# Two-layer attention and RWKV trunk on one core: RWKV's key norms and small functions made during the input projection, its small projections in pairs, its inputs finished tile by tile

## The chip, the cores and the metric

One Trainium2 chip, one NeuronCore. The time is device microseconds (us) of one launch of the whole program. Everything is float32. Shares of TensorE's clock are of 2.4 GHz: 1.00 in a row is 2.4 GHz, 0.50 is 1.2 GHz.

## The reference, cut to what matters

Two layers over T = 1040 tokens of width 1024 (kept transposed: 8 tiles of 128 partitions by W = 1044 columns). Each layer has one input projection `z = u @ w_in`, whose columns feed sparse attention (A) and RWKV-7 time mixing (B), an output projection, and an MLP. Part B's inputs, which the change is about:

```
zB = zB + (zB_prev - zB) * mu_l                  # token shift
r, k, v, xw, xa, xg = split(zB)                  # 512, 512, 512, 64, 64, 160 (+32 for v mixing in layer 1)
w = -softplus(-(w0 + tanh(xw) @ w2)) - 0.5;  decay = exp(-exp(w))
a = sigmoid(a0 + xa @ a2);   g = sigmoid(xg) @ g2
if layer 1: v = v + (v_first - v) * sigmoid(v0 + parts[6] @ v2)
kk = k * k_k;  kk = kk / max(norm(kk per head), 1e-12)
k = k * (1.0 + (a - 1.0) * k_a)
y = rwkv7_scan(r, decay, k, v, kk, kk * a)       # then group norm, bonus, gate by g
```

## The kernel before, in words

The program is written by hand, one instruction list per engine, with semaphores between them. A layer runs in this order: root mean square norm; the **projection**; **attention** by blocks of 128 queries; the **stage between** attention and the scan, which makes RWKV's inputs; the **scan** in 17 chunks of 64 tokens; the **stage behind** it (group norm, bonus, gate); the output projection; the MLP.

**Projection.** `z` has 24 tiles of 128 columns, called units u0 to u23; `ORDER` says which tile is made when. TensorE makes a unit with 24 matmuls (`unit`, 8 contraction tiles by 3 slices of 348 columns; each f32 matmul is two instructions in the trace) into three PSUM banks. There are two such triples of banks, used in turn by the list `ITEMS`, which holds the units and a few other products; an item waits until ScalarE has emptied the item two places before it (`tri_out`). ScalarE empties a unit that takes part in the token shift with two copies (`shifted`: one scaled by 1 - mu, one by mu into `stage`), and GpSimd adds the second, one token later, to the first (`add_shifted`).

Meanwhile VectorE searches the threshold of the 256 best keys per query, one bit at a time, 31 bits (`bit_step`): a few operations on 7 columns give the trial value (`trial_ready`), `count_ge` counts five blocks, and ScalarE counts the two longest ones (`sign_counts`: a Sign over 1024 and one over 1040 columns). ScalarE does its share of the bits behind certain units, by the table `BITS_AFTER` (2 or 3 bits behind each of units 12 to 19). ScalarE works in program order: while it waits for a bit it empties no PSUM.

Before the change u10 to u13 are the tiles of r, u14 to u17 k, u18 to u21 v, u22 the tile of xw and xa (`Z_LORA`), u23 that of xg. Attention may start when the last `add_shifted` is through (VectorE's wait on `z_ready`, then L1669 to L1673, then `attn_in`).

**Stage between.** All after attention (`attn_done`): VectorE scales k by k_k (L1722); ScalarE squares it (L1263) and makes tanh and two sigmoids (L1265 to L1269); TensorE makes four products for w (contraction over 64 rows, L974); then sums of squares per head (L985, 8 output rows); VectorE's max (L1737); ScalarE's inverse root as Ln and Exp (L1072, L1074); four products for a (64 rows) and in layer 1 four for v (32 rows); four products that spread the inverse norms over the head's rows (`one`, L671, 8 rows); VectorE multiplies (L1745), mixes v in layer 1 (L1735, L1749, L1750), and at the end treats k and kk over all four tiles at once (L1754, L1758, L1760). ScalarE empties each product with a sigmoid (L1279), two triples of banks in turn. The scan starts with ScalarE's L1142 (`scan_ready`).

**Stage behind.** Mean by blocks (L1007), squares, sums per head (L1015, the same 8-column selector), inverse root, bonus (L1025), gate (L1034 with 128 rows, L1036 with 32) and the spread of the inverse root (L1043, 8 rows). The selectors are loaded by DMA before each of the two stages (`heads_in`).

## Time and profile before

| | us |
|---|---|
| Median of 3 runs | 4003.57 (4001.94 to 4006.88) |
| The profiled execution, its own time | 3997.3 |
| Its span, first to last instruction | 3995.5 |
| TensorE busy | 3693.6 (92%) |
| VectorE busy | 2082.3 (52%) |
| ScalarE busy | 902.5 (23%) |
| GpSimd busy | 563.0 (14%) |
| Mean granted clock of TensorE | 0.949 |

The shares are means over stages with different limits, so they don't tell what the change is worth. A wait row reads "engine, line <- who was waited for: total us, times, longest us". In the timeline, the bracket at a row's end is the engine's idle time just before it and who ended it.

### The profile page before, as it was taken

To read this page: it belongs to the slowest core of one execution; us is meant where nothing else is said; L and a number is where in the kernel's file an instruction comes from. 1 tells how busy PE (TensorE), PEld (TensorE's weight loads), DVE (VectorE), ACT (ScalarE), POOL (GpSimd) and SP (SyncE) were. 2 spreads that over 40 slices of the span, in tenths; PEclk is the share of its full clock that TensorE was granted. 3 is DMA by queue.
4 is the path that set the end of the run, shared out by engine and by line. 5 is a ranking of instruction groups with operands and counts; after the bars stand their busy time and mean duration, and the time that the engine had idled before them with its cause. 6 is when DMAs were issued, how large, how long until landed. Compare 5 with 4: busy or idle time off the path is not lost.

```text
span 3995.5 us, 68805 instructions
## 1 busy us (share of the span) xinstructions
PE 3693.6 (92%) x29040; PEld 2815.2 (70%) x29040; DVE 2082.3 (52%) x4090; ACT 902.5 (23%) x1765; POOL 563.0 (14%) x444
## 2 busy tenths in 40 slices
PE   7999887999979999999899998869999799999996
PEld 5565554996658888888655665559956588888885
DVE  2499745775153242434536997357751532434345
ACT  2345562332020000000124446523320200000000
POOL 0131100000012222222101310000000222222220
PEclk9999996998989999999999999869989899999998
DMA  3110110000211111112211111100002111111121
GB/s 117 30 42 32 46 22 1 4 4 26 74 55 47 46 44 43 43 43 85 85 41 32 37 33 24 33 2 4 4 26 75 64 43 42 43 43 43 43 85 54
DMA packets 44408, 165.75 MB, mean 41 GB/s; under 512 B 5568, under 2 KB 5584, under 8 KB 43744
## 3 DMA queue, kind: packets, MB, share of 16 engines
q1 hardware_dynamic: 28672, 102.82, 7.8%
q0 software_dynamic: 15456, 58.78, 4.0%
q8 instruction: 227, 3.72, 0.4%
q14 instruction: 53, 0.43, 0.0%
HBM read 135.01 MB, written 23.49 MB: 40 GB/s over the span
## 4 chain that ended last, share of the span: by engine, by line
PE 79%; DVE 14%; issue 3%; ACT 3%; POOL 1%; DMA 0%; DVEq 0%; ACTq 0%; POOLq 0%
PE ps L737 39%; PE ps L686 10%; PE ps L763 10%; PE ps L654 6%; DVE arena L1455 4%; PE ps L932 2%; PE ps L920 2%; PE ps L945 1%; PE ps L974 1%; DVE little L1485 1%; PE ps L698 1%; DVE arena L1351 1%; PE ps L664 1%; DVE arena L1358 1%; ACT arena L1240 1%
## 5 line engine op out<-in xcount | busy, mean ns | idle before, releaser
L737 PE MATMUL ps<-arena 128*128 128x261 f32 x4096 | 924.7, 383 | 3.9 <-POOL arena L573 2.9
L737 PEld LDWEIGHTS ps<-arena 128*128 128x128 f32 x4096 | 775.1, 189 | 133.3 <-issue 4.6
L686 PE MATMUL ps<-arena,ring 128*128 128x348 f32 x2304 | 702.6, 464 | 34.4 <-ACT arena L1113 20.7
L737 PE MATMUL ps<-arena,ring 128*128 128x261 f32 x3072 | 711.6, 387 | 15.1 <-DVE arena L1822 14.4
L737 PEld LDWEIGHTS ps<-arena,ring 128*128 128x128 f32 x3072 | 587.2, 192 | 119.3 <-issue 13.9
L686 PEld LDWEIGHTS ps<-arena,ring 128*128 128x128 f32 x2304 | 437.7, 192 | 299.1 <-issue 49.3
L763 PE MATMUL ps<-arena 64*64 64x64 f32 (+1 forms) x13600 | 475.6, 225 | 70.9 <-DVE arena L1536 43.2
L763 PEld LDWEIGHTS ps<-arena 64*64 64x64 f32 x13600 | 450.9, 135 | 91.6 <-issue 45.5
L1311 ACT ACTIVATE aux<-ps 128x522 f32<-128x522 f32 x64 | 38.9, 607 | 1527.6 <-PE ps L737 1527.6
L1397 DVE TENSOR_TENSOR arena<-aux,ps 128x522 f32<-128x522 f32 x160 | 111.8, 699 | 423.9 <-PE ps L737 423.4
L573 POOL TENSOR_TENSOR arena<-ring 128x512 f32<-128x512 f32 x128 | 172.4, 1347 | 1098.3 <-DMA ring<-units 1092.9
L1455 DVE TENSOR_SCALAR_CACHE_REDUCE arena<-arena,little 128x384 uint8<-128x384 f32 (+6 forms) x338 | 278.9, 885 | 11.2 <-DVE little L1479 11.0
L1397 DVE TENSOR_TENSOR arena<-arena,ps 128x522 f32<-128x522 f32 x200 | 139.8, 699 | 239.6 <-PE ps L737 237.1
L654 PE MATMUL ps<-arena,ring 128*128 128x348 f32 x768 | 228.5, 461 | 3.7 <-issue 3.7
L654 PEld LDWEIGHTS ps<-arena,ring 128*128 128x128 f32 x768 | 147.6, 193 | 85.6 <-issue 8.3
L1136 ACT ACTIVATE arena<-arena,little 128x1024 bf16<-128x1024 f32 x124 | 142.2, 1147 | 206.3 <-DVEq L1480 206.1
L546 POOL TENSOR_TENSOR arena<-arena 128x1043 f32<-128x1043 f32 x30 | 72.9, 2431 | 531.2 <-ACTq L1115 531.2
L1154 ACT ACTIVATE arena<-ps 128x128 f32<-128x128 f32 x340 | 92.8, 277 | 231.1 <-PE ps L763 217.5
L1688 DVE CUSTOM_DVE_ANT_0 arena<-ps,arena 128x128 f32<-128x128 f32 (+7 forms) x130 | 94.0, 760 | 94.6 <-PE ps L920 84.6
L1340 DVE TENSOR_TENSOR aux<-arena 128x1044 f32<-128x1044 f32 x16 | 19.9, 1246 | 194.1 <-ACT arena L1097 194.1
L1402 DVE SCALAR_TENSOR_TENSOR arena<-arena 128x522 f32<-128x522 f32 (+1 forms) x96 | 101.9, 1062 | 14.5 <-DVE arena L1397 1.1
L1601 DVE TENSOR_TENSOR arena<-arena,ps 128x128 f32<-128x128 f32 x340 | 95.5, 286 | 24.2 <-PE ps L763 23.8
(217 smaller groups left out, 3530.6 us busy)
## 6 DMA issues: line engine op xcount, KB each, us to landing
ring<-units SPq DMA_DIRECT2D x192, 512.0 KB, 3.7
h_scratch<-arena POOLq DMA_DIRECT2D x24, 522.0 KB, 3.3
arena<-h_scratch POOLq DMA_DIRECT2D x24, 522.0 KB, 8.0
arena<-h_in POOLq DMA_DIRECT2D x16, 522.0 KB, 9.9
out<-arena POOLq DMA_DIRECT2D x8, 522.0 KB, 3.2
arena<-att_scratch POOLq DMA_DIRECT2D x2, 2080.0 KB, 9.1
att_scratch<-arena POOLq DMA_DIRECT2D x16, 256.0 KB, 3.0
aux<-rope POOLq DMA_DIRECT2D x2, 1044.0 KB, 12.3
```

Source lines behind the costliest of these rows:

```text
L573: nc.gpsimd.tensor_tensor(w_sum(p, i), x, y, op).then_inc(S["weights_ready"], 1)
L654: ins = mm(ps[:, b + s, 0:SW], ring[:, (u % RING) * D + k * P:(u % RING) * D + (k + 1) * P], rhs(g * KT + k)[:, slice_(s)], start=(g == 0 ...
L686: ins = mm(ps[:, b + s, 0:SW], ring[:, r * D + k * P:r * D + (k + 1) * P], tile(U0, k)[:, slice_(s)], start=(k == 0), stop=(k == KT - 1))
L737: ins = mm(acc_at(n)[:, s], lhs[:, k * P:(k + 1) * P], rhs(k)[:, s * HALF:(s + 1) * HALF], start=(k == 0), stop=(k == KT // 2 - 1))
L763: ins = mm(out[r:r + HEAD], lhs[r:r + HEAD], rhs[r:r + HEAD], start=start, stop=stop)
L1136: go(signs[j][0:n], sc(b)[0:n], ACT.Sign, bias=negated[0:n, j:j + 1], scale=1.0, accum_out=sel[0:n, c:c + 1]).then_inc(S["signs_counted"], 1)
L1154: go(cb("x", 256)[:, P * half:P * (half + 1)], ps[:, half, 0:P], ACT.Copy).then_inc(S["x_out"], 1)
L1397: do(v.tensor_tensor(o, x, y, ALU.add))
L1402: do(v.scalar_tensor_tensor(x, x, 0.0, x, ALU.max, ALU.mult))
L1455: v.tensor_scalar(junk[j % 3][0:n, 0:SEL_W[b]], sc(b)[0:n], trial[0:n, c], None, ALU.is_ge, ALU.add, accum_out=count[0:n, c]).then_inc(S[" ...
L1601: v.tensor_tensor(mt, mt, bank2(2, 5, half), ALU.subtract).then_inc(S["mt_ready"], 1)
L1688: v.tensor_tensor_reduce(sm[u % 2][r][:, 0:k], flat[:, c:c + k], mask, -HEAD ** -0.5, 3.0e38, ALU.add, ALU.min, stat[:, at:at + 1])\
```

## The change

- The order of the units: u10 is the tile of xw and xa, u11 that of xg, u12 to u15 are k, u16 to u19 v, u20 to u23 r.
- Behind unit 13's bits ScalarE makes tanh and the sigmoids; behind those of units 14 to 17 it squares k (scaled by k_k, into the room of r). A new item "kk" behind u18 (`pair_sums`, 12 matmuls of 32 output rows, tile g into PSUM rows 32g to 32g+31) sums the squares per head; ScalarE copies it out behind unit 18's bits, VectorE takes the max behind the bits of unit 18, ScalarE makes the inverse root behind unit 20's copies.
- Between attention and the scan, each tile g: the products for w (rows 0 to 63) and a (rows 64 to 127) alternate into banks 0 to 2 and 3 to 5; the inverse norm is spread in two halves of 522 columns into banks 6 and 7, from 32 rows; VectorE makes kk from k, k_k and PSUM in one operation per half, scans the decay, and scales k and a; the factor 1 + (a - 1) k_a moves to ScalarE.
- The selectors (`selectors`, 128 by 160) lie in SBUF for good: a third DMA before h is loaded, and the two `heads` DMAs of each layer go. The stage behind uses them too, with 32 rows where 8 were.

```diff
-ORDER = [Z_KI, Z_QI, Z_QI + 1, Z_MISC, Z_C, Z_C + 1, *range(Z_Q, NZ)]
+ORDER = [Z_KI, Z_QI, Z_QI + 1, Z_MISC, Z_C, Z_C + 1, *range(Z_Q, Z_R), Z_LORA, Z_XG, *range(Z_K, Z_LORA), *range(Z_R, Z_K)]
-         *(f"u{n}" for n in range(9, NZ)))
+         *(f"u{n}" for n in range(9, 19)), "kk", *(f"u{n}" for n in range(19, NZ)))
...
+            def pair_sums(l):
+                b = tri_bank("kk")
+                pe.wait_ge(tri("kk"), tri_out(l, "kk") - 1)
+                pe.wait_ge(S["kk_sq"], 4 * (l + 1))
+                for s in range(SLICES):
+                    for g in range(4):
+                        ins = mm(of_pair(ps, g)[:, b + s, 0:SW], pair_sum, z(Z_R + g)[:, slice_(s)], start=True, stop=True)
+                ins.then_inc(S["virt_done"], 1)
...
+                    if n == 18:
+                        pair_sums(l)
...
+                for g in range(4):
+                    if g:
+                        pe.wait_ge(S["lora_out"], outs + 2 * g)
                     for s in range(SLICES):
-                        ins = mm(ps[:, b + s, 0:SW], a, x[:, slice_(s)], start=True, stop=True)
+                        for b, h in ((0, slice(0, 64)), (SLICES, slice(64, P))):
+                            ins = mm(ps[:, b + s, 0:SW], ax("w2a2")[h, g * P:(g + 1) * P], z(Z_LORA)[h, slice_(s)],
+                                     start=True, stop=True)
                     ins.then_inc(S["lora_ready"], 1)
+                    for half in range(2):
+                        if g or half or l:
+                            pe.wait_ge(S["kk_out"], 8 * l + 2 * g + half)
+                        for j in range(2):
+                            at = half * SPLIT + j * HALF
+                            ins = mm(ps[:, 6 + j, 0:HALF], of_pair(selectors, g)[:, PAIR:PAIR + P],
+                                     of_pair(kk_rows, g)[:, at:at + HALF], start=True, stop=True)
+                        ins.then_inc(S["kk_ready"], 1)
...
+                    if n == 13:
+                        act.wait_ge(S["z_ready"], mixed(11))
+                        go(z(Z_LORA)[0:64], z(Z_LORA)[0:64], ACT.Tanh)
+                        go(z(Z_XG), z(Z_XG), ACT.Sigmoid)
+                        go(z(Z_MISC)[0:32], z(Z_MISC)[0:32], ACT.Sigmoid).then_inc(S["lora_in"], 1)
+                    if 14 <= n < 18:
+                        g = n - 14
+                        act.wait_ge(S["z_ready"], mixed(K_UNIT + g))
+                        go(z(Z_R + g), z(Z_K + g), ACT.Square, scale=par(l, "kk", g)).then_inc(S["kk_sq"], 1)
+                    if n == 18:
+                        act.wait_ge(S["virt_done"], virt_at(l, "kk"))
+                        go(thirds(kk_rows), banks(tri_bank("kk")), ACT.Copy).then_inc(tri("kk"), 1)
...
+                    if n == 20:
+                        act.wait_ge(S["kk_max"], w.next("kk_max"))
+                        inverse_root(kk_rows, kk_rows, 0.0, 1).then_inc(S["root_ready"], 1)
...
+                for g in range(4):
+                    act.wait_ge(S["lora_ready"], w.next("lora_ready"))
+                    for b, dst, name in ((0, X_S0, "w0"), (SLICES, X_A0, "a0")):
+                        go(thirds(tile(dst, g, W, ZW)), banks(b), ACT.Sigmoid, bias=par(l, name, g), scale=1.0)\
+                            .then_inc(S["lora_out"], 1)
+                    act.wait_ge(S["lora_out"], outs + 2 * g + 2)
+                    go(yv(g), tile(X_A0, g, W, ZW), ACT.Identity, scale=par(l, "ka", g), bias=omka[:, g:g + 1])\
+                        .then_inc(S["ka_ready"], 1)
...
                 for g in range(4):
+                    kk, s, a, k = (tile(base, g, W, ZW) for base in (X_KK0, X_S0, X_A0, Z0 + Z_K * ZW))
+                    for half in range(2):
+                        part = slice(half * SPLIT, (half + 1) * SPLIT)
+                        dve.wait_ge(S["kk_ready"], w.next("kk_ready"))
+                        v.scalar_tensor_tensor(halves(kk[:, part]), halves(k[:, part]), par(l, "kk", g), ps[:, 6:8, 0:HALF],
+                                               ALU.mult, ALU.mult).then_inc(S["kk_out"], 1)
+                    scan = tile(X_S0, g, ZW, ZW)
+                    dve.wait_ge(S["lora_out"], outs + 2 * g + 1)
+                    v.tensor_tensor_scan(scan, const("reset"), scan, 0.0, ALU.mult, ALU.add).then_inc(S["dve_done"], 1)
...
+                    v.tensor_tensor(k, k, yv(g), ALU.mult).then_inc(S["keys_scaled"], 1)
+                    v.tensor_tensor(a, a, kk, ALU.mult).then_inc(S["dve_done"], 1)
```

**VectorE, from the end of attention (L1716, in the changed kernel L1740) to the first chunk.** Before:

```order
L1716 TENSOR_TENSOR arena<-ps,arena 128x512
L1722 TENSOR_SCALAR arena<-arena,prm 128x1088 x4
L1724 TENSOR_SCALAR little<-prm 128x4
L1729 MEMSET arena 128x44
L1730 SCALAR_TENSOR_TENSOR arena<-cst,arena 128x1088
L1737 TENSOR_SCALAR arena<-ps 8x1044
L1741 MEMSET arena 128x4x44
L1745 TENSOR_TENSOR arena<-arena,ps 128x1044 x4
L1754 TENSOR_SCALAR arena<-arena,prm,little 128x1044 x4
L1758 TENSOR_TENSOR arena<-arena 128x4x1044
L1760 TENSOR_TENSOR arena<-arena 128x4x1044
```

(The L1729 and L1730 rows stand there four times.) Now, the first tile of four and the end:

```order
L1740 TENSOR_TENSOR arena<-ps,arena 128x512
L1748 MEMSET arena 128x4x44 x2
L1754 SCALAR_TENSOR_TENSOR arena<-arena,prm,ps 128x522 x2
L1758 SCALAR_TENSOR_TENSOR arena<-cst,arena 128x1088
L1762 TENSOR_TENSOR arena<-arena 128x1044
L1763 TENSOR_TENSOR arena<-arena 128x1044
L1765 MEMSET arena 128x4x44
L1777 MEMSET arena 128x256
```

The four passes over all tiles have become one pass per tile, and the max over the sums is gone from here.

**ScalarE, in the projection of the changed kernel, from behind unit 13's bits to the copies of unit 15.** L1114 and L1118 are the two copies of a unit, L1141 the Signs, L1239 to L1241 tanh and sigmoids, L1245 a square:

```order
L1239 ACTIVATE arena<-arena 64x1044
L1240 ACT_TABLE_LOAD
L1240 ACTIVATE arena<-arena 128x1044
L1241 ACTIVATE arena<-arena 32x1044
L1114 ACTIVATE arena<-ps,arena 128x1044
L1118 ACTIVATE arena<-ps,prm 128x1044
L1141 ACTIVATE arena,little<-arena,little 128x1024
L1141 ACTIVATE arena,little<-arena,little 16x1040
L1141 ACTIVATE arena,little<-arena,little 128x1024
L1141 ACTIVATE arena,little<-arena,little 16x1040
L1245 ACTIVATE arena<-arena,prm 128x1044
L1114 ACTIVATE arena<-ps,arena 128x1044
```

Before, L1109 and L1113 (the copies) and L1136 (the Signs) stood there alone, in the same order. The Signs behind the sigmoids need no table of their own.

**TensorE, in the projection of the changed kernel, from unit 9 on.** L683 are the units' matmuls, 24 to a unit, L714 the pair sums:

```order
L683 MATMUL ps<-arena,ring 128x348 x240
L714 MATMUL ps<-arena,selectors 32x348 x12
L683 MATMUL ps<-arena,ring 128x348 x120
L929 MATMUL ps<-arena 128x128 x4
```

Before it was one row of 360 (units 9 to 23): the pair sums now stand between unit 18 and unit 19.

## Rows read from the trace of the kernel before

**Rows 1.** The page's first line.

```profile
span 3995.5 us, 68805 instructions
```

**Rows 2.** Chain that ended last, layer 0: start, length, what.

```profile
568.30 1.92 PE ps L920 x8
...
590.15 10.43 issue
600.58 14.27 PE ps L974 x24
...
616.06 9.54 PE ps L985 x24
...
640.02 14.30 PE ps L671 x24
...
949.32 7.13 PE ps L1015 x24
```

**Rows 3.** Timeline: both layers' stage between, its first and last row.

```profile
590.27 0.69 DVE L1716 TENSOR_TENSOR arena<-ps,arena 128x512 f32<-128x512 f32 x1 [6.32 <-ACT arena L1249]
...
668.35 0.42 ACT L1142 ACTIVATE arena<-arena 128x256 f32<-128x256 f32 x1 [27.08 <-DVEq L1764]
...
2557.14 0.69 DVE L1716 TENSOR_TENSOR arena<-ps,arena 128x512 f32<-128x512 f32 x1 [6.32 <-ACT arena L1249]
...
2659.47 0.42 ACT L1142 ACTIVATE arena<-arena 128x256 f32<-128x256 f32 x1 [37.17 <-DVEq L1764]
```

**Rows 4.** Busy time by stretch; the column behind POOL is TensorE's granted clock.

```profile
37.00:62.00 25.00, 24.93 (x80) 16.04 (x81) 11.41 (x11) 1.04 (x1) 0.00 (x0) 0.93 0.06 22
560.00:590.00 30.00, 26.31 (x288) 19.47 (x285) 8.29 (x16) 19.03 (x35) 1.44 (x2) 1.00 0.04 12
601.00:615.00 14.00, 13.84 (x24) 7.37 (x23) 7.33 (x6) 3.52 (x4) 0.00 (x0) 0.50 0.00 0
970.00:1009.00 39.00, 37.97 (x61) 15.63 (x59) 12.55 (x10) 4.16 (x4) 0.00 (x0) 0.53 0.00 0
```

**Rows 5.** Timeline of the projection's last bits and units, layer 0.

```profile
397.38 1.15 ACT L1136 ACTIVATE arena<-arena,little 128x1024 bf16<-128x1024 f32 x1 [3.00 <-DVEq L1480]
...
402.76 1.15 ACT L1136 ACTIVATE arena<-arena,little 128x1024 bf16<-128x1024 f32 x1 [3.00 <-DVEq L1480]
...
405.05 1.11 ACT L1109 ACTIVATE arena<-ps,arena 128x1044 f32<-128x1044 f32 x1
...
406.07 1.11 ACT L1113 ACTIVATE arena<-ps,prm 128x1044 f32<-128x1044 f32 x1
...
407.23 28.35 PE L686 MATMUL ps<-arena,ring 128*128 128x348 f32 x96 [2.85 <-ACT arena L1113]
...
407.29 2.40 POOL L546 TENSOR_TENSOR arena<-arena 128x1043 f32<-128x1043 f32 x1 [15.88 <-ACTq L1115]
407.36 2.36 DVE L1485 SCALAR_TENSOR_TENSOR little<-little,cst 128x7 int32<-128x7 int32 x1
...
440.48 0.27 DVE L1669 MEMSET arena<- 128x256 f32 x1 [12.54 <-POOL arena L546]
```

**Rows 6.** Single lines: count, duration in ns min/median/max.

```profile
L1267 ACT ACT_TABLE_LOAD  x2: 1283/1283/1283, 597.0 to 2563.8; - x2
L1279 ACT ACTIVATE arena<-ps,prm x20: 1122/1130/1131, 604.4 to 2619.9; 128x1044 f32<-128x1044 f32 x20
L1730 DVE TENSOR_TENSOR_SCAN arena<-cst,arena x8: 2424/2424/2426, 605.8 to 2583.1; 128x1088 f32<-128x1088 f32 x8
L1745 DVE TENSOR_TENSOR arena<-arena,ps x8: 1241/1242/1244, 644.0 to 2635.4; 128x1044 f32<-128x1044 f32 x8
```

**Rows 7.** Timeline: a VectorE count while GpSimd adds, layer 0.

```profile
255.01 2.40 POOL L557 TENSOR_TENSOR arena<-arena 128x1044 f32<-128x1044 f32 x1
...
255.13 0.61 DVE L1455 TENSOR_SCALAR_CACHE_REDUCE arena<-arena,little 128x384 uint8<-128x384 f32 x1 [0.17 <-DVE little L1479]
```

**Rows 8.** Groups of instructions by form: busy us, mean ns.

```profile
L1397 DVE TENSOR_TENSOR arena<-aux,ps 128x522 f32<-128x522 f32 x160 | 111.8, 699 | 423.9 <-PE ps L737 423.4 <-DVE arena L1381 0.4
```

More of the change, by code:

```diff
@@ L130 @@
 X_ROWS0 = X_KK0 + 4 * ZW
[L131 to L134 removed]
+assert X_VF0 + 3 * T <= Z0 and X_ROWS0 + W <= ARENA
+PAIR = P // 4
 MIX0 = Z0 + Z_R * ZW
@@ L980, in _ @@
-                pe.wait_ge(S["lora_out"], w.value("lora_out", 2))
-                pe.wait_ge(S["heads_in"], 16 * (2 * l + 1))
-                for g in range(4):
-                    pe.wait_ge(S["kk_sq"], w.next("kk_sq"))
-                    for s in range(SLICES):
-                        ins = mm(ps[0:HEADS, s, 0:SW], head_sum(g), yv(g)[:, slice_(s)], start=(g == 0), stop=(g == 3))
-                ins.then_inc(S["kk_sums"], 1)
-                pe.wait_ge(S["kk_max"], w.next("kk_max"))
-                for g in range(4):
-                    lora(ax("w2a2")[64:128, g * P:(g + 1) * P], z(Z_LORA)[64:128])
+                    for half in range(2):
[6 more added lines that the diff above has]
+                        ins.then_inc(S["kk_ready"], 1)
@@ L990, in _ @@
                 if l:
                     for g in range(4):
-                        lora(ax("g2b")[32:64, g * P:(g + 1) * P], z(Z_MISC)[32:64])
-                pe.wait_ge(S["lora_out"], w.value("lora_out", 2))
-                pe.wait_ge(S["root_ready"], 6 * l + 2)
-                for g in range(4):
-                    one(head_spread(g), head_rows, SLICES * (g % 2), "kk_out", "kk_ready")
+                        pe.wait_ge(S["lora_out"], outs + 7 + g)
+                        b = SLICES * (g % 2)
@@ L998, in _ @@
+                        for s in range(SLICES):
+                            ins = mm(ps[:, b + s, 0:SW], ax("g2b")[32:64, g * P:(g + 1) * P], z(Z_MISC)[32:64, slice_(s)],
+                                     start=True, stop=True)
+                        ins.then_inc(S["lora_ready"], 1)
                 pe.wait_ge(S["rwkv_in"], w.next("rwkv_in"))
@@ L1267, in _ @@
-                go(z(Z_XG), z(Z_XG), ACT.Sigmoid).then_inc(S["act_done"], 1)
-                act.wait_ge(S["act_done"], w.next("act_done"))
-                go(z(Z_MISC)[0:32], z(Z_MISC)[0:32], ACT.Sigmoid).then_inc(S["act_done"], 1)
-                act.wait_ge(S["act_done"], w.next("act_done"))
-                act.sem_inc(S["lora_in"], 1)
-                outs = [(dst, name, g) for dst, name in ((X_S0, "w0"), (X_A0, "a0"), (X_Y0, "v0"))[:3 if l else 2]
-                        for g in range(4)]
@@ new lines, in _ @@
+                    for b, dst, name in ((0, X_S0, "w0"), (SLICES, X_A0, "a0")):
[4 more added lines that the diff above has]
+                        .then_inc(S["ka_ready"], 1)
+                if l:
+                    for g in range(4):
+                        act.wait_ge(S["lora_ready"], w.next("lora_ready"))
+                        act.wait_ge(S["keys_scaled"], 4 * l + g + 1)
+                        go(thirds(yv(g)), banks(SLICES * (g % 2)), ACT.Sigmoid, bias=par(l, "v0", g), scale=1.0)\
+                            .then_inc(S["lora_out"], 1)
@@ L1661, in _ @@
                 first_step()
-                for bit in range(BITS):
-                    bit_step(l, bit)
+                searched = 0
+                for after, bits in BITS_AFTER.items():
+                    for bit in range(searched, searched + bits):
+                        bit_step(l, bit)
+                    searched += bits
+                    if after == 18:
+                        dve.wait_ge(S["kk_sums"], w.next("kk_sums"))
+                        v.tensor_scalar(kk_rows, kk_rows, 1e-24, None, ALU.max).then_inc(S["kk_max"], 1)
                 last_step()
```

123 lines of the change are left out of this document (43 added, 80 removed).

## The prediction

> **What bounds the kernel now.** The span is 3995.5 us [rows 1], 1.8 us less than the profiled execution's own 3997.3; the median of the runs is 4003.57, 6.3 us above that. I work out a difference and take it from both. The chain of waits is read first, since a mean share tells nothing of stages. In the stage between it never lies on work that needs the machine [rows 2]: 10.4 us in which TensorE waits for ScalarE's squares, tanh and sigmoids, 14.3 us for four products of 64 rows, 9.5 us for sums with 8 output rows, 14.3 us for four spreads from 8 rows. The timeline gives the stage's length, from the end of L1716 to the scan's first operation [rows 3]: 590.96 to 668.35 is 77.4 us in layer 0, 2557.83 to 2659.47 is 101.6 us in layer 1. The stretches give the clock [rows 4]: 1.00 through attention, 0.50 at 601 to 615, where TensorE is busy 13.8 of 14 us but with matmuls of 64 of the 128 rows, and 0.53 in the gate stretch (128, 32 and 8 rows by turns).
>
> The other place is the projection [rows 5]. VectorE's search sets its pace: one bit takes 5.38 us (402.76 less 397.38), of which ScalarE's Signs are 2.4 and 3.0 are waiting. A unit's copies (405.05, 406.07) take 2.2 us, then GpSimd's add runs 2.4 us, and VectorE's small operation L1485 that meets it takes 2.36 us, which is 0.2 elsewhere: 2.1 us lost per unit. Two units carry 5 bits, 5 x 5.38 + 2 x 2.13 = 31.2 us, against TensorE's 28.35 for two units; hence the wait of 2.85 at 407.23. The last two units have no bits: TensorE runs 407.23 to 435.6 and attention starts at 440.48, after VectorE stood 12.5 us. So whatever delays TensorE's last units delays everything, and VectorE has 12.5 us to spare.
>
> **What the change costs in the projection.** ScalarE first. Behind unit 13's bits come tanh, a table load and two sigmoids: 1.28 for the load, some 1.1 for each operation on 1044 columns [rows 6], 4.5 us. VectorE's next bit needs ScalarE 3.6 us before it is there; 1.7 of it is covered by VectorE's own counts, so the search loses 2.0 us, once. The four squares add 1.06 us each in front of a unit's copies; ScalarE has 3.0 us to spare there. They do something else: the GpSimd add starts 1.06 us later, at 5.5 us into a step instead of 4.5, when VectorE's small operations (4.2 to 5.3) are over, and meets the counts. A count of 384 columns that ran beside a GpSimd operation took 0.61 us, its usual time [rows 7]. So from unit 14 on a unit loses the 2.1 us no more.
>
> TensorE does worse. Before, unit 19 started when unit 17's banks were empty, near 359. Now the item kk stands between units 18 and 19, and needs the fourth square, which ScalarE makes only behind unit 17's three bits. Step by step in layer 0. Before, the copies of unit 20 start at 405.05 [rows 5]; counted back by 31.2 for two units, those of unit 18 start at 373.9 and those of unit 14 at 311.1. Now: unit 14 at 311.1 + 4.5 = 315.6; unit 15 after two bits, 311.1 + 2 x 5.38 + 2.0 (the search's loss) + 1.06 (the square) = 324.9; unit 16 after three, 341.1; unit 17 after two, 351.9; three bits and the fourth square, 368.1. TensorE gets the banks of unit 16 at 343.3, or what it has queued through a little later (its units 16 and 17 start 4.6 us late, with a short spell at 1.2 GHz): unit 18 ends between 360.5 and 362.2, and TensorE stands 6 to 8 us. The pair sums are 24 instructions. Unhidden bounds: 9.5 us if one after the other (L985) [rows 2], 2.4 if four at a time; nearest is the pair of L920 in attention, 8 instructions of 512 columns in 1.92 us, where 348 columns alone take 7.13 / 24 = 0.297 and 512 thus 0.437: 1.8 at a time. At the start of the program TensorE, fresh from a wait, shows 0.93 over 25 us, some 3.5 us at 1.2 GHz [rows 4]; I expect that here. I take 4 us, near the pair's value. Unit 19 then starts at 372.3, five units of 14.18 follow without a wait (ScalarE is behind none of them), and TensorE ends at 443.2 instead of 435.6. With the small operation that moves in front of attention (0.2), **+7.8 us a layer, +15.6** in all; by the bounds +6 to +13.5 a layer. ScalarE's inverse root behind unit 20 and VectorE's max (0.8) lie under these units.
>
> The Trainium skill ("ScalarE: Activation LUTs", What ACT_TABLE_LOAD costs) puts a switch of tables at about 2.66 us with a drain. The rows show 1283 ns; by the page's figure the sigmoids end 1.4 us later and the sum is 2.8 us worse for both layers.
>
> The Trainium skill ("TensorE: Matmul & The Clock Gate", Measured speedup vs the span model) gives 2.38 for three column tiles. An estimate by it: 24 x 0.58 / 2.38 = 5.8 us for the pair sums at the low clock, 3.6 us worse for both layers. No row has four column tiles.
>
> **What it saves in the stage between.** From the end of L1716 on. TensorE needs only that, since tanh, sigmoids and roots are done; it was at work until 590.15 [rows 2], so the first tile runs at full clock. Both products of a tile, 12 instructions: at L920's 1.8 at a time 2.0 us, at 1.2 GHz 4.0 (14.27 / 4 = 3.6 for one product). A half spread, 4 instructions of 261 columns: 14.30 / 24 x 0.75 x 4 = 1.8 at 1.2 GHz and some 0.35 until VectorE has it; 1.1 and less at full clock. VectorE per tile: two halves from PSUM of 0.70 (the row of 522 columns [rows 8]), scan 2.42, two multiplications of 1.24 [rows 6]. First tile: 2.2 + 1.1 + 0.7 + 1.2 + 0.7 + 2.4 + 2.6 = 11.0. Each later one: 0.7, then 2.2 until the second half is there (banks 6 and 7 must be empty), 0.7, 2.4, 2.6: 8.7. TensorE has 4.0 + 2.2 for the next tile beside the last 5.7 of that, so it is as late as VectorE: 8.8. I use the low clock for them, since products of 64 rows without a pause went at 0.50 at 601 to 615 [rows 4] and here TensorE has pauses as well; at full clock a tile takes 7.8. ScalarE's three operations (3.4) lie beside. Memsets 1.1. Layer 0: 11.0 + 26.4 + 1.1 = 38.5, **38.9 less** than 77.4. Layer 1 adds 12 operations of 1.27 for v, 15.3; its four products (14) run beside: 53.8, **47.8 less** than 101.6.
>
> Stage behind: sums of squares change column tiles only every 6 instructions, so they stay near 7.13; the two DMAs there ended before they were needed. -1 a layer. Start: one DMA issue more ahead of h, +0.5.
>
> Sum: 15.6 - 38.9 - 47.8 - 2 + 0.5 = -72.6. The profiled execution would be 3924.7, the median **3931**. What a measurement tells from no change is 0.2%, 8 us.
>
> **The rivals.**
> 1. Forecast: -72, in its own range -62 to -84 (clock in the tiles, pair sums). Chance 0.65.
> 2. The projection pays more: pair sums one after the other, and the GpSimd adds still meet small operations (margin 0.2 us by the rows), so the fourth square comes at 374: +13 to +19 a layer, -50 to -61. For it: nothing measured on four column tiles. Chance 0.14.
> 3. The pairs don't overlap: each tile waits for 7.2 + 2.2, 3.3 more, seven tiles' worth: -50. L920 speaks against it, though it has other lengths. 0.05.
> 4. The clock holds at 2.4 GHz in the gate stretch, because 32 rows stand where 8 did: its 39 us [rows 4], about as many in layer 1, would halve but for a few us: some 35 us more off, -107. Against it: the products of 64 rows alone stood at 0.50 [rows 4], and most of this stretch's matmuls are the same as before. 0.09.
> 5. The moved work comes back in full: TensorE stands another 36 us in each projection. That needs a wait in the middle that VectorE's search prolongs by 7 bits; the steps above show one of 8. -8 to +8: 0.02.
> 6. Slower: TensorE stays at 1.2 GHz after its wait at the pair sums. Each unit then costs 14.2 more; five in each layer are 142, +70. It decides from 2.6 units a layer on. Against it: full-row matmuls came back to full clock within some 3.5 us at the start [rows 4]. 0.03, with whatever else would delay the search.
>
> The remaining 0.02 lies faster than any. The range must hold 8 in 10: 0.65 of the first and most of the second and third, a little of the fourth: 3915 to 3954. Faster by over 0.2%: 0.95; within: 0.02; slower: 0.03.
>
> **What would show it.** In the profile after: the stage between 38 to 40 us and 53 to 56 us, with VectorE's four tiles 8 to 9 us apart and TensorE's clock near 0.5 to 0.6 in it; a TensorE wait of 6 to 8 us before the pair sums, released by ScalarE's square, and the pair sums at 4 us; the last unit's end 7 to 8 us later; L1485's counterpart short at units 15 to 18; the gate stretch at 0.53 still. I'm wrong if the wait stands elsewhere, if the pair of products takes 7 us, or if the projection ends at its old time.

## The result, and the profile after

The changed kernel took 3915.59 us (median of 4, 3905.09 to 3919.16) against 4002.76 of the kernel before in the same series (4000.59 to 4006.88): a ratio of 0.9777, 95% interval 0.9756 to 0.9797. It is faster, by 87 us where 73 were forecast. The profiled execution took 3913.9 us, 83.4 less than that of before; its page begins so (the second line is the granted clock in 40 slices):

```profile
span 3912.0 us, 68853 instructions
...
PEclk9999998998989999999999999979979899999998
```

To find the miss I cut both traces at four places: VectorE's first operation of attention (L1669 before, L1693 after), its memset of the scan's state (L1761, L1777), TensorE's first group-norm mean (L1007, L1013) and its first matmul of the output projection. Lengths in us:

| stretch | before | after | difference | forecast |
|---|---|---|---|---|
| start to attention, layer 0 | 440.48 | 448.58 | +8.1 | +8.3 |
| attention and stage between, layer 0 | 227.24 | 186.06 | -41.2 | -38.9 |
| scan, layer 0 | 274.31 | 274.64 | +0.3 | 0 |
| stage behind, layer 0 | 67.79 | 61.69 | **-6.1** | -1 |
| layer 0's output projection to layer 1's attention | 1396.52 | 1403.24 | +6.7 | +7.8 |
| attention and stage between, layer 1 | 252.50 | 203.74 | -48.8 | -47.8 |
| scan, layer 1 | 273.25 | 274.09 | +0.8 | 0 |
| stage behind, layer 1 | 67.87 | 62.18 | **-5.7** | -1 |
| rest | 995.54 | 997.78 | +2.2 | 0 |

The differences sum to -83.5. The forecast -72.6 misses 11 us, and two stretches, the stages behind the scan, hold 9.8 of them. (The medians lie 87 us apart; the four times of the changed kernel spread over 14 us.)

**Projection.** The timeline of the kernel after, layer 0, answers to [rows 5] (start, length, engine, line; in brackets the idle time ahead and what ended it):

```profile
282.84 28.35 PE L683 MATMUL ps<-arena,ring 128*128 128x348 f32 x96 [1.64 <-ACT arena L1118]
...
318.33 44.41 PE L683 MATMUL ps<-arena,ring 128*128 128x348 f32 x144 [7.15 <-ACT arena L1118]
...
368.75 3.71 PE L714 MATMUL ps<-arena,selectors 128*32 128x348 f32 x24 [6.01 <-ACT arena L1245]
...
372.38 71.07 PE L683 MATMUL ps<-arena,ring 128*128 128x348 f32 x240
...
448.29 0.17 DVE L1692 TENSOR_SCALAR little<-prm 128x4 f32<-128x4 f32 x1 [26.45 <-POOL arena L545]
448.58 0.27 DVE L1693 MEMSET arena<- 128x256 f32 x1
```

TensorE waits 6.0 us for the fourth square (L1245), the pair sums take 3.7, and the units end at 443.45. No small operation of VectorE's search between 300 and 372 takes over 0.23 us any more; before the change four there took 2.4 us. Look at two more things. At unit 15 there is a wait of 7.15 us, and VectorE now stands 26.45 us ahead of attention instead of 12.5. Both matter below. The busy time by stretch shows the clock around the two waits (the column behind POOL, as in [rows 4]):

```profile
316.00:320.00 4.00, 1.67 (x3) 1.18 (x4) 3.12 (x8) 3.88 (x6) 1.60 (x1) 0.50 0.00 2
...
323.00:326.00 3.00, 3.00 (x11) 1.90 (x10) 3.00 (x7) 3.00 (x6) 0.00 (x0) 1.00 0.00 0
...
370.00:374.00 4.00, 4.00 (x24) 1.61 (x17) 3.77 (x11) 3.02 (x5) 2.45 (x1) 0.54 0.00 0
374.00:378.00 4.00, 4.00 (x15) 2.63 (x14) 3.66 (x12) 2.07 (x3) 0.00 (x0) 1.00 0.00 0
```

Finely cut, the clock is 0.50 from 318.33 to 322.4 and from 368.75 to 373.6, so for 4.1 and 4.9 us behind the ends of the waits, and 0.99 in the some 4 us that follow each.

**Stage between.** The timeline of TensorE in layer 0: L984 are the 12 instructions of a tile's two products, L992 a half spread.

```profile
600.53 2.02 PE L984 MATMUL ps<-arena,aux 64*128 64x348 f32 x12 [1.87 <-DVEq L1743]
602.48 1.14 PE L992 MATMUL ps<-aux,selectors 32*128 32x261 f32 x4
604.55 1.14 PE L992 MATMUL ps<-aux,selectors 32*128 32x261 f32 x4 [0.93 <-DVE arena L1754]
606.13 3.50 PE L984 MATMUL ps<-arena,aux 64*128 64x348 f32 x12 [0.44 <-ACT arena L1289]
...
621.45 3.85 PE L984 MATMUL ps<-arena,aux 64*128 64x348 f32 x12
```

The first pair of products takes 2.02 us at the full clock, the later ones 3.4 to 3.85; VectorE's tiles are 7.3 to 8.3 us apart.

**Stage behind.** The same view, and the gate stretch's clock. L1020 are the group-norm sums, L1041 the gate's products of 32 rows, L1048 the spread:

```profile
916.50 4.45 PE L1020 MATMUL ps<-arena,selectors 128*32 128x348 f32 x24
...
952.75 1.53 PE L1039 MATMUL ps<-arena,aux 128*128 128x348 f32 x2
954.20 0.94 PE L1041 MATMUL ps<-arena,aux 32*128 32x348 f32 x1
954.21 0.94 PE L1048 MATMUL ps<-arena,selectors 32*128 32x348 f32 x1
...
966.02 3.10 PE L1048 MATMUL ps<-arena,selectors 32*128 32x348 f32 x5
...
934.00:970.00 36.00, 35.12 (x62) 13.99 (x61) 12.40 (x10) 4.16 (x4) 0.00 (x0) 0.54 0.00 0
```

The sums went from 7.13 us [rows 2] to 4.45. A spread's first instruction starts at 954.21, beside the gate's last but one (954.20), and its other five take 3.10 us. Before the change a spread's six instructions followed the gate's and took:

```profile
992.07 3.68 PE L1043 MATMUL ps<-arena 8*128 8x348 f32 x6
```

The clock stayed low, 0.54 against 0.53 [rows 4].

### The profile page after: what moved, and what is told of

Its sections match the earlier page's. It is cut to its first block, busy times and chain, and to the rows that moved or that the text cites. A ratio compares the mean times of both kernels' runs of the same rounds, so it can differ in the third digit from the quotient of the medians.

```text
span 3912.0 us, 68853 instructions
## 1 busy us (share of the span) xinstructions
PE 3642.7 (93%) x29056; PEld 2796.3 (71%) x29056; DVE 2040.8 (52%) x4090; ACT 914.8 (23%) x1775; POOL 562.8 (14%) x441
## 4 chain that ended last, share of the span: by engine, by line
PE 70%; DVE 9%; ACT 2%; issue 2%; POOL 0%; DVEq 0%; ACTq 0%; POOLq 0%
PE ps L744 40%; PE ps L770 10%; PE ps L651 6%; PE ps L683 6%; DVE arena L1472 2%; DVE arena L1368 1%; PE ps L941 1%; PE ps L929 1%; DVE arena L1375 1%; PE ps L954 1%; PE ps L1041 1%; PE ps L1039 1%; PE ps L661 1%; PE ps L695 1%; DVE arena L1838 1%
## 5 line engine op out<-in xcount | busy, mean ns | idle before, releaser
L683 PE MATMUL ps<-arena,ring 128*128 128x348 f32 x2304 | 700.7, 463 | 31.3 <-ACT arena L1118 17.6
L683 PEld LDWEIGHTS ps<-arena,ring 128*128 128x128 f32 x2304 | 437.7, 192 | 295.3 <-issue 50.6
L770 PE MATMUL ps<-arena 64*64 64x64 f32 (+1 forms) x13600 | 477.1, 225 | 48.3 <-DVE arena L1564 23.6
L1328 ACT ACTIVATE aux<-ps 128x522 f32<-128x522 f32 x64 | 38.9, 607 | 1527.6 <-PE ps L744 1527.6
L1141 ACT ACTIVATE arena<-arena,little 128x1024 bf16<-128x1024 f32 x124 | 142.2, 1147 | 161.6 <-DVEq L1497 159.9
```

The source lines that it names most:

```text
L683: ins = mm(ps[:, b + s, 0:SW], ring[:, r * D + k * P:r * D + (k + 1) * P], tile(U0, k)[:, slice_(s)], start=(k == 0), stop=(k == KT - 1))
L770: ins = mm(out[r:r + HEAD], lhs[r:r + HEAD], rhs[r:r + HEAD], start=start, stop=stop)
L1141: go(signs[j][0:n], sc(b)[0:n], ACT.Sign, bias=negated[0:n, j:j + 1], scale=1.0, accum_out=sel[0:n, c:c + 1]).then_inc(S["signs_counted"], 1)
```

## The experiments

Fourteen kernels ran, each timed beside the kernel before, whose median lay between 4000.3 and 4004.3. "Over the changed kernel" compares medians with 3915.6, which was measured in its own series. Since the changed kernel's times spread over 14 us and the medians of before over 4, a difference of 10 us or less in these medians is not clear of noise; there the lengths of stretches and instructions in the traces carry the reading.

A product writes some rows of PSUM and reads some rows of its operands. Sets of 32 rows written are called column tiles here, sets of 32 or 64 rows read are row tiles.

**1 and 2. Is the stage behind's gain the overlap of products in different rows?** The first kernel puts all sums in one column tile and all spreads in one row tile (and makes the inverse root from that tile's 32 rows), the second only the spreads.

```diff
-  ins = mm(of_pair(ps, g)[:, s, 0:SW], pair_sum, tile(X_KK0, g, W, ZW)[:, slice_(s)],
+  ins = mm(of_pair(ps, 0)[:, s, 0:SW], pair_sum, tile(X_KK0, g, W, ZW)[:, slice_(s)],
...
-  ins = mm(ps[:, s, 0:SW], of_pair(selectors, g)[:, PAIR:PAIR + P], of_pair(gn_rows, g)[:, slice_(s)],
+  ins = mm(ps[:, s, 0:SW], of_pair(selectors, 0)[:, PAIR:PAIR + P], of_pair(gn_rows, 0)[:, slice_(s)],
```

> The changed kernel, but behind the scan all four pairs' group-norm sums are written to output rows 0 to 31, one over the other, and all four spreads read the selectors and the rows 0 to 31. So the group norm uses the last pair's sums for every pair; the number and the shapes of TensorE's instructions stay the same. Theory 1: instructions that touch different rows of PSUM or of the operand run beside each other although the rows change only every six instructions, and that is what the stage behind the scan gained beyond the forecast. Then the sums go from 4.4 back to about 7.1 us and the spreads of tiles 1 to 3 from 2.3 to about 3.5 us each: 2.7 + 3.4 = 6.1 us a layer, 12 us in all over the changed kernel. Theory 2: the gain comes from the new shape (32 output columns and no accumulation in place of 8 with it, 32 operand rows in place of 8). Then the time is that of the changed kernel within 1 us.

Measured: 3927.26 us (ratio 0.9811, 0.9798 to 0.9825), 12 over the changed kernel. In its timeline the sums are back, and so is a spread:

```profile
916.70 7.21 PE L1020 MATMUL ps<-arena,selectors 128*32 128x348 f32 x24
...
946.88 3.68 PE L1048 MATMUL ps<-arena,selectors 32*128 32x348 f32 x6
```

The stage behind is 67.4 and 68.3 us long, as before the change (67.8, 67.9). TensorE's instructions have the changed kernel's shapes, so the shape is not the cause.

> The changed kernel, but the four spreads behind the scan all read the selectors and the rows 0 to 31, the same rows that the gate's 32-row products in front of them read. So the group norm uses the first pair's sums for every pair; the sums are made as in the changed kernel. Theory 1 (different rows run beside each other): the spreads of tiles 1 to 3 go from 2.3 to about 3.5 us, 3.4 us a layer and 7 us in all over the changed kernel. Theory 2 (the shape): no difference, within 1 us. Theory 3 (TensorE's time in the gate stretch is hidden behind VectorE): the spreads get longer by the 3.4 us, the whole time by less than 2 us.

Measured: 3920.55 us (0.9799, 0.9785 to 0.9812), 5 over, which alone would show nothing. The stage is 65.9 and 65.2 us, 4.2 and 3.1 longer; the sums stay at 4.45, a spread takes 3.68. The 3.4 us of Theory 1 are there in both layers, so it holds in both kernels, and the longer spreads are on the path.

**3. The alternating products of the stage between.**

```diff
-  for s in range(SLICES):
-      for b, h in ((0, slice(0, 64)), (SLICES, slice(64, P))):
+  for b, h in ((0, slice(0, 64)), (SLICES, slice(64, P))):
+      for s in range(SLICES):
```

> The changed kernel, but in the stage between attention and scan the six products of one tile are issued as three of the first half's rows and then three of the second half's, not alternating. Theory 1 (in this stage TensorE sets the tiles' distance, and the alternating order makes the pairs overlap): 12 products, 2.0 us at the full clock and 3.4 to 3.9 us at the low one, come near 3.6 and 7 us, or less where three against three still overlap in part, so 5 to 12 us a layer, 10 to 24 us in all. Theory 2 (the change every three instructions overlaps as well as the change every one): within 2 us. Theory 3 (ScalarE's and VectorE's chain of a tile sets the distance of 7.3 to 8.3 us): products longer, time within 2 us.

Measured: 3927.93 us (0.9812, 0.9799 to 0.9825), 12 over; attention and stage between are 8.3 and 2.2 us longer. TensorE of this kernel, layer 0:

```profile
600.74 2.68 PE L984 MATMUL ps<-arena,aux 64*128 64x348 f32 x12 [1.87 <-DVEq L1743]
...
617.09 5.17 PE L984 MATMUL ps<-arena,aux 64*128 64x348 f32 x12
```

2.68 and 5.17 us in place of 2.02 and 3.4 to 3.85: a change every three products overlaps in part, a change at each one more. At the low clock the tiles now stand 10.1 us apart. Run 5, with the alternating order and the low clock, has 8.8 us, with a pair of products of 3.85: the 1.3 us more are the products' own, so TensorE sets this distance. Three such distances are 4 of layer 0's 8.3 us. The rest goes with the clock, 0.56 in this stage against 0.73, and layer 1's 2.2 us lie within what this code varies by (last section).

**4. The stage behind alone, in the kernel before.** Its selectors get 160 more columns, and:

```diff
-  ins = mm(ps[0:HEADS, s, 0:SW], head_sum(g), tile(X_KK0, g, W, ZW)[:, slice_(s)],
-           start=(g == 0), stop=(g == 3))
+  ins = mm(of_pair(ps, g)[:, s, 0:SW], pair_sum, tile(X_KK0, g, W, ZW)[:, slice_(s)],
+           start=True, stop=True)
...
-  ins = mm(ps[:, s, 0:SW], head_spread(g), head_rows[:, slice_(s)], start=True, stop=True)
+  ins = mm(ps[:, s, 0:SW], of_pair(pair_spread, g), of_pair(gn_rows, g)[:, slice_(s)], start=True, stop=True)
```

> The kernel before, with only the stage behind the scan changed: group-norm sums of pair g in output rows 32g, each sum by itself, spreads from the rows 32g; the selectors for it come with the second load of the old ones. Theory 1: the stage's gain is its own, 6.1 and 5.7 us of the two layers: 12 us under the kernel before, a ratio of 0.997. Theory 2: the gain depends on the rest of the change (the clock in front of the stage, the selectors kept resident): 2 us or less. The forecast on record would give 2 us.

Measured: 3994.56 us against 4002.78, a ratio of 0.9979 (0.9970 to 0.9988), so 5 to 12 us faster. The stage is 61.9 and 60.9 us, 5.9 and 7.0 shorter than before, and the sums take what they take in the changed kernel:

```profile
951.27 4.45 PE L1024 MATMUL ps<-arena 128*32 128x348 f32 x24
```

The gain is this stage's own: Theory 1.

**5 to 7. What holds TensorE in the projection?** The forecast had the small functions delay ScalarE, and the pair sums wait for the fourth square. The first of these kernels moves the small functions, the second the pair sums, the third both (the copy of the sums, the maximum and the root move along):

```diff
-                    if n == 13:
+                    if n == 21:
                         act.wait_ge(S["z_ready"], mixed(11))
                         go(z(Z_LORA)[0:64], z(Z_LORA)[0:64], ACT.Tanh)
```

```diff
-         *(f"u{n}" for n in range(9, 19)), "kk", *(f"u{n}" for n in range(19, NZ)))
+         *(f"u{n}" for n in range(9, 20)), "kk", *(f"u{n}" for n in range(20, NZ)))
...
-                    if n == 18:
+                    if n == 19:
                         pair_sums(l)
```

> The changed kernel, with ScalarE's tanh and its two sigmoids (and the table load in front of them) issued behind unit 21's copies in place of unit 13's. Theory 1 (the forecast's step): the 4.5 us that they take make TensorE wait 7.15 us in place of some 2.9 at unit 15 and push all behind it; ScalarE has free time behind unit 21. Then that wait falls to about 3 us, and the projection ends 4 to 5 us earlier in each layer, 8 to 10 us in all. Theory 2: the end of the projection is set by the search, whose steps wait for VectorE and not for these functions: the wait moves to a later unit and the time stays within 2 us.

Measured: 3916.65 us (0.9785, 0.9771 to 0.9798), no difference. Its TensorE, and the one long small operation of its search:

```profile
314.41 44.43 PE L683 MATMUL ps<-arena,ring 128*128 128x348 f32 x144 [2.87 <-ACT arena L1118]
369.51 3.64 PE L714 MATMUL ps<-arena,selectors 128*32 128x348 f32 x24 [10.68 <-ACT arena L1245]
...
314.55 2.37 DVE L1502 SCALAR_TENSOR_TENSOR little<-little,cst 128x7 int32<-128x7 int32 x1
```

The waits went from 7.15 + 6.01 to 2.87 + 10.68. The fourth square starts at 368.22, in the changed kernel at 367.45: without the small functions GpSimd's addition meets VectorE's small operation again, and the search is as late as before. Theory 2.

> The changed kernel, with the pair sums of the squares issued behind unit 19 in place of unit 18 (their copy, VectorE's maximum and the inverse root move with them). Theory 1 (the forecast's step): TensorE's 6.0 us wait ahead of the pair sums is for the fourth square, which is there long before unit 19 ends; the wait goes and nothing takes its place: 5 to 6 us a layer, 10 to 12 us in all. Theory 2: the next units then wait for ScalarE's copies behind the same search steps, and half or more of the wait comes back: 0 to 6 us in all.

Measured: 3909.49 us (0.9764, 0.9751 to 0.9777), 6 less than the changed kernel. The 6.0 us are gone, and waits of 1.7 and 2.9 us stand at the next two units: Theory 2 here as well. Attention starts 1.9 us earlier in layer 0.

> The two moves together: pair sums behind unit 19, the small functions behind unit 21. Theory 1 (two waits, each by itself): the gains add up, 9 to 10 us a layer, so 18 to 20 us in all, and TensorE ends the projection about as early as in the kernel before plus the pair sums' 3.7 us. Theory 2 (one cause behind both: ScalarE is late by the small functions when it comes to the fourth square): the gain is that of the better of the two moves alone, 10 to 12 us. Theory 3 (the search is the bound): 6 us or less.

Measured: 3906.68 us (0.9756, 0.9742 to 0.9769), 9 less than the changed kernel, between what Theories 2 and 3 give; attention starts 3.1 us earlier in layer 0. A wait of 6.4 us now stands behind the pair sums. In layer 0, from unit 15 on, TensorE waits 13.2 us in the changed kernel and 13.6, 11.8 and 9.6 in these three: moving the work takes away a part of the wait at best. Wherever it goes, ScalarE stands in the search's steps.

**8. Gate and spread products by turns.** In each tile the 128-row products first, then:

```diff
+  for s in range(SLICES):
+      ins = mm(ps[:, s, 0:SW], of_pair(selectors, g)[:, PAIR:PAIR + P], of_pair(gn_rows, g)[:, slice_(s)],
+               start=True, stop=True)
+      last = mm(ps[:, 3 + s, 0:SW], ax("g2b")[0:32, g * P:(g + 1) * P], z(Z_MISC)[0:32, slice_(s)],
+                start=False, stop=True)
```

> The changed kernel, but in the gate stretch each tile's three 128-row products come first, and then the gate's 32-row products and the spread's, alternating. Theory 1: as they read different rows (in tiles 1 to 3), six of the one and six of the other run beside each other, where now only the last one or two of the gate's do; at the stretch's lower clock, 0.73 us each, some 2 us a tile are gained, 4 to 6 us a layer, 8 to 12 us in all, and the tiles' distance falls from 11.1 to about 9 us. Theory 2: VectorE's chain of a tile (two products, an addition) sets the distance once TensorE is faster, or the wait for the PSUM banks ahead of the spread now also holds the gate's products: within 2 us, or slower.

Measured: 3885.81 us (0.9704, 0.9691 to 0.9717), 30 less than the changed kernel: three times what the overlap was to give. The stage is 48.3 us long in both layers, and tiles are 6.7 us apart. In the timeline six instructions of 128 rows take 3.5 us. Then the pairs of gate and spread instructions start 0.29 us apart, half of that pace, at the full clock (1.00 from 948.5 to 950.5):

```profile
944.98 3.60 PE L1039 MATMUL ps<-arena,aux 128*128 128x348 f32 x6 [1.17 <-ACT arena L1318]
948.51 0.56 PE L1045 MATMUL ps<-arena,selectors 32*128 32x348 f32 x1
948.51 0.56 PE L1047 MATMUL ps<-arena,aux 32*128 32x348 f32 x1
948.90 0.45 PE L1045 MATMUL ps<-arena,selectors 32*128 32x348 f32 x1
...
934.00:955.00 21.00, 17.54 (x54) 9.38 (x52) 11.56 (x9) 3.12 (x3) 0.00 (x0) 0.76 0.00 1
```

From the gate's first instruction to the last spread it is 25.7 us at a clock of 0.80, in the changed kernel 39.1 us at 0.59. The overlap was foreseen, the clock was not.

**9. Another table of search steps.** ScalarE's share of the search is spread evenly and ends a unit later:

```diff
-BITS_AFTER = {8: 1, "val": 3, 9: 2, 10: 2, 11: 3, 12: 2, 13: 3, 14: 2, 15: 3, 16: 2, 17: 3, 18: 2, 19: 3}
+BITS_AFTER = {8: 1, "val": 3, 9: 2, 10: 2, 11: 3, 12: 2, 13: 2, 14: 2, 15: 2, 16: 2, 17: 2, 18: 3, 19: 2, 20: 3}
```

> The changed kernel with another table for the 31 search steps: two behind each of units 12 to 17 and 19, three behind 18 and 20, in place of two and three in turn up to 19. So the search ends a unit later; VectorE then waits 26 us for GpSimd in front of attention, which hides it. Theory 1 (what makes TensorE wait 7.15 us at unit 15 and 6.0 us at the pair sums is ScalarE standing in the search's steps, wherever the small functions are): the waits fall to 0 to 3 us, the projection ends some 10 to 13 us earlier in each layer, 20 to 26 us in all. Theory 2 (the forecast's step: the small functions, 4.5 us once, and GpSimd's additions behind the squares make the waits): two thirds of them stay, 8 us or less in all.

Measured: 3881.32 us (0.9704, 0.9691 to 0.9717), 34 less than the changed kernel. Attention starts at 432.07 instead of 448.58. The small functions and the squares are where the change put them, and TensorE hardly waits:

```profile
311.86 42.39 PE L683 MATMUL ps<-arena,ring 128*128 128x348 f32 x144 [1.77 <-ACT arena L1118]
354.18 1.96 PE L714 MATMUL ps<-arena,selectors 128*32 128x348 f32 x24
356.49 70.47 PE L683 MATMUL ps<-arena,ring 128*128 128x348 f32 x240 [0.35 <-ACT arena L1118]
...
340.00:380.00 40.00, 39.65 (x154) 24.92 (x153) 36.07 (x107) 25.59 (x37) 7.29 (x3) 1.00 0.12 40
```

Of the 16.5 us of layer 0, 11.0 are the waits (7.15 - 1.77 + 6.01, less 0.35), 4.4 the clock that no longer falls behind them (44.41 - 42.39, 3.71 - 1.96, 71.07 - 70.47), and 1.1 an earlier start of this part. That is Theory 1's cause, and more than it gave, since it had left the clock out. From layer 0's output projection to layer 1's attention the gain is 15.0 us.

**10. The gate in blocks.** The 128-row products, then the 32-row ones, then the spread:

```diff
   for s in range(SLICES):
       mm(ps[:, 3 + s, 0:SW], ax("g2a")[:, g * P:(g + 1) * P], z(Z_XG)[:, slice_(s)], start=True, stop=False)
+  for s in range(SLICES):
       ins = mm(ps[:, 3 + s, 0:SW], ax("g2b")[0:32, g * P:(g + 1) * P],
                z(Z_MISC)[0:32, slice_(s)], start=False, stop=True)
```

> The changed kernel, but in each tile of the gate stretch the three 128-row products come first, then the gate's three 32-row ones, then the spread as before. This splits the 13.9 us a layer that the run with alternating 32-row products gained where 4 to 6 were expected. Theory 1 (TensorE loses time at each change between 128 and 32 rows: 0.73 us a record in the mix against 0.58 us in a block of one kind, at the same clock): 12 records cost some 7 us in place of 8.8, the tiles' distance falls from 11.1 to 8.5 to 9.3 us, 7 to 10 us a layer, 14 to 20 us in all. Theory 2 (the gain came from spread and gate products side by side and from the clock, which then rose): 2 us a layer or less, 4 in all.

Measured: 3881.88 us (0.9691, 0.9677 to 0.9706), 34 less than the changed kernel; the stage is 44.6 and 47.9 us long in place of 61.7 and 62.2. One tile of its timeline, and the stretch from the gate's first instruction to the last spread:

```profile
943.22 2.02 PE L1039 MATMUL ps<-arena,aux 128*128 128x348 f32 x6 [0.44 <-ACT arena L1319]
945.17 1.14 PE L1042 MATMUL ps<-arena,aux 32*128 32x348 f32 x3
945.87 0.56 PE L1049 MATMUL ps<-arena,selectors 32*128 32x348 f32 x1
946.15 0.45 PE L1042 MATMUL ps<-arena,aux 32*128 32x348 f32 x1
946.26 0.45 PE L1049 MATMUL ps<-arena,selectors 32*128 32x348 f32 x1
...
930.93:952.99 22.06, 21.18 (x73) 12.18 (x71) 12.83 (x11) 3.79 (x4) 0.00 (x0) 0.92 0.00 1
```

The same stretch of the changed kernel:

```profile
930.00:969.12 39.12, 39.12 (x73) 15.56 (x71) 12.83 (x11) 4.16 (x4) 0.00 (x0) 0.59 0.00 0
```

Run 10's timeline shows the mechanism of overlap: the spread's first instruction starts at 945.87, with three of the gate's six instructions still to start (946.15, 946.45 and the next), and from there both run side by side. At one and the same clock, blocks are also cheaper than the mix. In tile 0, at 1.00 in both kernels, the gate's 12 instructions take 4.5 us mixed (930.00 to 934.48) and 3.7 in blocks (930.93 to 934.63). But most is the clock. An estimate: length times granted clock is 23.1 us in the changed kernel (39.12 x 0.59) and 20.3 in run 10 (22.06 x 0.92), so of the 17 us of layer 0 some 3 are the order and the overlap, and 14 the clock. In layer 1 the stretch takes 25.3 us at 0.80. So Theory 1's effect is there, but it is the smaller part. Theory 2's 4 us in all were far too few, although the clock that it named is the larger part. Runs 8 and 10 show that the order decides how the clock is granted; why it does stays open.

**11 and 12. The two together, and the moves on top.**

> The alternating gate and spread products and the spread table of the search together. If the two gains are independent they add up: 30 us of the first (3885.8) and what the table alone gives, so about 3862 if that is 24 us, and 3878 if it is 8.

Measured: 3850.33 us (0.9628, 0.9615 to 0.9641), 65 less than the changed kernel, where 30 + 34 are 64: the gains add up.

> As the run before this one, and the pair sums behind unit 19 and the small functions behind unit 21 too. If the table has taken TensorE's waits away, the moves give nothing more: within 3 us of the run before. If a wait at the pair sums is left, they give 3 to 8 us more.

Measured: 3852.64 us (0.9635, 0.9622 to 0.9648). The moves give nothing once the table has taken the waits.

**13. The table in the kernel before.**

> The kernel before, with only the other table of search steps. Its TensorE waits 11.7 us for ScalarE in five waits of at most 2.9 us in layer 0's projection, at a clock of 0.99. Theory 1 (what the table gives is the wait and, where a wait is 6 us or longer, the lower clock behind it, which the kernel before has hardly any of): TensorE starts attention 7 to 9 us earlier in each layer, 14 to 18 us in all, half of what the changed kernel gained by it (34 us); then the moved work costs the projection next to nothing once the search does not hold TensorE. Theory 2 (the table's gain does not depend on the change): 30 us or more.

Measured: 3980.05 us (0.9947, 0.9933 to 0.9960), 21 less than before. The two stretches up to attention hold 16 of them, which is Theory 1 (14 to 18). Of this kernel's projection nine units (48 instructions each) are one row without a wait:

```profile
282.56 126.63 PE L686 MATMUL ps<-arena,ring 128*128 128x348 f32 x432 [1.66 <-ACT arena L1113]
```

Attention starts at 430.98, 9.5 us earlier than before the change, against 16.5 in the changed kernel; from layer 0's output projection to layer 1's attention it gains 6.8 against 15.0. So with the even table, kernels without and with the change start attention at 430.98 and 432.07, and in the second stretch they take 1389.7 and 1388.2 us.

**14. The best version:** the even table and the gate in blocks.

> The gate's products in blocks and the spread table of the search together, the gains of the two single runs (34 us each) if they add up: 3847 to 3850 us. The stretches that the two touch lie apart, so that only the clock could couple them; with less than 60 us together, a low clock has moved to another stretch.

Measured: 3847.54 us, 0.9608 of the kernel before (0.9595 to 0.9621), 68 less than the changed kernel: 34 + 34. It is faster than the kernel before and the changed one. Its gate stretch is 23.7 us long at a clock of 0.86 in layer 0, and 20.4 at 1.00 in layer 1.

## Why the prediction was right, and where it was wrong

**Faster, and mainly by the mechanism named: right.** Attention and the stage between gave 89.9 us in the two layers, where 86.7 were forecast. The miss is small: the ratio 0.9777 of the 4003.57 from which the forecast started is 3914.3, just under its range of 3915 to 3954.

**Projection: the sum right, two of its reasons off.** +14.8 us measured in the two stretches up to attention, +16.1 forecast. In layer 0 the copies of units 14 to 17 start at 316.16, 325.42, 341.58 and 352.35 (forecast 315.6, 324.9, 341.1, 351.9), the wait is 6.0 (6 to 8), the pair sums 3.7 (4), TensorE's end 443.45 (443.2). Two points were off. The forecast put the pair sums at 1.8 at a time, 4 us at the full clock; they ran at 1.96 us for 24 at the full clock (run 9), 3.7 at a time, and took 3.71 only since the clock was low behind the wait. The two errors cancel, so this term came out by luck. And the small functions were booked as part of the price, while run 5 shows that taking them away gives nothing. What costs is that ScalarE is in a search step when TensorE needs it (run 9). With the even table the change costs the projection 1.1 us in layer 0 instead of 8.1.

The table load took 1.28 us in this place too (312.92), and the sigmoid behind it started at 314.22. The Trainium skill ("ScalarE: Activation LUTs", What ACT_TABLE_LOAD costs) has about 2.66 us with a drain; the trace shows no more than the 1.3. The Trainium skill's factor for three column tiles ("TensorE: Matmul & The Clock Gate", Measured speedup vs the span model), 2.38, was put against four tiles in the forecast as the dearer case; the runs show 3.7 for four (7.21 / 1.96).

**Stage between: right, a little too dear.** Layer 0 came out 2.3 us better and layer 1 1.0 better than forecast. The pair of products took 2.02 us at the full clock as forecast (2.0), and 3.4 to 3.85 at the low one (4.0). The rest goes with the clock: the forecast held it low for all later tiles; over the stage it was 0.73 in layer 0. The runs in which this stretch was not touched show how far that moves the time (stretch from the first product to the state's memset, layer 0, of runs 6 and 5):

```profile
598.30:632.10 33.80, 21.51 (x80) 12.00 (x80) 24.82 (x23) 16.20 (x14) 0.67 (x1) 0.76 0.03 8
...
600.60:638.10 37.50, 27.27 (x80) 14.52 (x80) 24.92 (x24) 16.19 (x14) 0.67 (x1) 0.61 0.02 7
```

VectorE's busy time is the same, and at 0.76 the stretch is 33.8 us, at 0.61 37.5. In layer 1 it is 53.6 at 0.57 (run 6) and 48.7 at 0.67 (run 5). What moves the clock within identical code stays open.

**Stage behind: wrong.** This is the step that failed: "sums of squares change column tiles only every 6 instructions, so they stay near 7.13", and with it "-1 a layer". Measured were -6.1 and -5.7. The sums fell by 2.7 us, to 4.45: they overlap although their column tile changes only every six instructions. The spreads, not counted at all, overlap with the gate's 32-row products in tiles 1 to 3: 3.10 us for five instead of 3.68 for six, and the first one beside the gate's. The last tiles stand 11.1 us apart in place of 12.2, so three of them give the other 3.4 us. Runs 1, 2 and 4 show it from both sides: with the same row tile and column tile the time is back, and in the kernel before the same edit brings the gain. That an instruction of the next tile starts ahead of the last one's rest is seen in run 10, where the two have lines of their own; for the sums it is a reading.

**The rivals.** The second and third fell: the additions met no small operation, and the pairs overlap. The fourth, a full clock in the gate stretch, did not come with the change (0.54), but its price was real. Run 10 brought the clock of the gate stretch to 0.92 and 0.80 by the order alone and gained 34 us where the rival had put 35, a smaller part of it by the overlap and the blocks. The fifth fell. The sixth came in small: the clock was low behind the wait, and was back at 374.

## What to carry to other kernels

Products that read different rows of their operands, or write different rows of PSUM, overlapped even where the rows change only every few instructions (7.2 us became 4.45), so a new layout of rows has to be looked at wherever it is used, also beside other lines' products. Where one engine works through a search's steps in program order, the table of those steps decides what any item placed between them costs: look for slack on the far side (26 us of VectorE here) and even the table out before moving work around. Try products of 128 and of 32 rows in blocks before mixing them, and count a wait of TensorE with the slow stretch behind it.

## What the runs showed of the hardware that was not expected

- Four column tiles, changed at each product: 24 instructions in 1.96 us at the full clock, 3.71 behind a wait, where 24 in one tile take 7.21. Changed every six: 4.45.
- Behind waits of 7.15 and 6.01 us the granted clock stood at 0.50 for another 4.1 and 4.9 us; behind the first TensorE's next 144 instructions took 44.41 us in place of 42.39. A short wait can cost the same: 44.43 us behind one of 2.87 us (run 5), while the 96 behind one of 2.85 [rows 5] ran at the full pace.
- Instructions of 128 and 32 rows mixed two by two take 0.37 us each at the full clock and 0.73 at the low one, in blocks 0.31 (run 10) and, those of 128 rows at a clock of 0.54, 0.59 (run 8). The clock over the whole stretch was 0.59 and 0.58 for the mix, in the two layers, and 0.92 and 0.80 for the blocks (run 10).
- A low clock in one place can leave or come while the code there is the same: layer 1's attention and stage between together took 199.2 to 205.4 us in runs 2, 5 to 8 and 10 to 12. Up to the stage's first product they all take 150.5 to 151.9 us; from there it is 48.7 us at a clock of 0.67 (run 5) to 53.6 at 0.57 (run 6).
